# Issuing a differential-attention step's scores ahead of the value matmuls of the step two before it

## The reference, cut to what matters

```python
h = rms_norm(x, norm_w) * (1 + scale(c)) + shift(c)
u_a, v_a, z_a, q_b, k_b, v_b, z_b = split(h @ w_in)      # 2048 x 3584
a_out = gmlp_spatial_gating(u_a, v_a, ...) * silu(z_a)
# differential attention: 4 heads, each with two q/k parts of 64 and values of 128
q, k = rope(rms_norm(q_b)), rope(rms_norm(k_b))
s = q @ k.T * 64 ** -0.5 ; s = where(causal, s, -inf)     # for both parts
p = softmax(s)
a = p[part 0] - lam * p[part 1]
o = rms_norm(a @ v_b, subln_w) * (1 - lambda_init)
b_out = o * silu(z_b)
x = x + gate(c) * (concatenate([a_out, b_out]) @ w_out)
```

## Time and profile before

| | |
|---|---|
| time, median of 3 runs (lowest to highest) | 626.02 us (625.65 to 626.02) |
| the profiled execution's own time | 625.31 us |
| its span on the slowest core, core 1 | 624.3 us |
| spans of the other cores | 618.0 to 621.4 us |
| granted TensorE clock, core 1 / others, mean | 0.929 / 0.920 to 0.959 |
| TensorE busy with matmuls | 463.1 us (74%) |
| VectorE busy | 341.8 us (55%) |
| ScalarE busy | 319.5 us (51%) |
| exponentials (line 885) | 144, 155.9 us busy, 44.8 us idle before them |
| value matmuls (line 895) | 1088, 90.1 us busy, 33.7 us idle before them |
| score matmuls (line 848) | 576, 57.5 us busy, 21.7 us idle before them |

### The profile page before, as it was taken

One profiled execution on the slowest core, in us unless ns is written; L12 is line 12 of the kernel. 1 busy time (PEld: TensorE's weight loads), 2 busy tenths in 40 slices (PEclk: granted clock), 3 DMA queues, 4 the chain that ended last, 5 costly groups with the idle time before them and its releaser, 6 DMA issues.

```text
span 624.3 us, 9650 instructions; the slowest of 8 cores (618.0 to 624.3 us)
## 1 busy us (share of the span) xinstructions
PE 463.1 (74%) x3232; PEld 230.9 (37%) x3232; DVE 341.8 (55%) x755; ACT 319.5 (51%) x416; POOL 33.6 (5%) x38
## 2 busy tenths in 40 slices
PE   0022269999999999998986887587578768849990
PEld 0000024444444434344433454355355435424440
DVE  2153792156628878744687335633734644475555
ACT  1140557555336766762224888588679849600000
POOL 2010000000000000000453000000000000000000
PEclk9997569999999999999899999789989979979996
DMA  8999950312722040050002600000000000044777
GB/s 216 300 243 286 326 88 2 46 23 101 169 34 36 1 67 2 2 101 1 1 2 51 120 2 1 2 2 2 1 2 2 2 1 2 2 135 135 241 263 236
DMA packets 21696, 50.64 MB, mean 81 GB/s; under 512 B 1424, under 2 KB 8848, under 8 KB 21648
## 3 DMA queue, kind: packets, MB, share of 16 engines
q1 hardware_dynamic: 12656, 39.22, 19.3%
q0 software_dynamic: 8992, 10.81, 11.2%
HBM read 51.40 MB, written 8.39 MB: 96 GB/s over the span
## 4 chain that ended last, share of the span: by engine, by line
PE 47%; DMA 16%; DVE 14%; ACT 12%; issue 9%; SPq 1%; DVEq 1%; ACTq 0%
PE psum L666 17%; PE psum L613 9%; ACT sb_regA L885 8%; PE psum L895 7%; DVE sb_regD L559 4%; PE psum L848 4%; DMA sb_szb<-xT 3%; DMA out<-sb_regD 3%; DVE sb_regB L932 3%; DMA sb_regA<-xT 3%; DMA out<-sb_regA 3%; DMA sb_regD<-x 2%; PE psum L973 2%; PE psum L712 2%; DVE sb_regB L914 2%
## 5 line engine op out<-in xcount | busy, mean ns | idle before, releaser
L885 ACT ACTIVATE sb_regA<-psum,sb_small 128x1024 bf16<-128x1024 f32 x144 | 155.9, 1112 | 44.8 <-PE psum L848 26.1
L666 PE MATMUL psum<-sb_hT,sb_regC 128*128 128x512 bf16 x512 | 118.8, 385 | 5.2 <-ACT sb_hT L433 5.2
L895 PE MATMUL psum<-sb_vB,sb_regA 128*128 128x129 bf16 x1088 | 90.1, 226 | 33.7 <-ACT sb_regA L885 25.7
L895 PEld LDWEIGHTS psum<-sb_vB,sb_regA 128*128 128x128 bf16 x1088 | 67.7, 100 | 64.7 <-issue 64.5
L613 PE MATMUL psum<-sb_regC,sb_hT 128*128 128x512 bf16 x384 | 88.3, 383 | 0.0
L666 PEld LDWEIGHTS psum<-sb_hT,sb_regC 128*128 128x128 bf16 x512 | 50.5, 99 | 64.6 <-issue 9.8
L848 PE MATMUL psum<-sb_qT,sb_kT 64*128 64x256 bf16 (+1 forms) x576 | 57.5, 279 | 21.7 <-DVE sb_hT L870 16.0
L409 PE MATMUL psum<-sb_vB,sb_constb 128*128 128x512 bf16 x32 | 14.3, 626 | 67.0 <-ACT sb_vB L405 67.0
L613 PEld LDWEIGHTS psum<-sb_regC,sb_hT 128*128 128x128 bf16 x384 | 37.4, 99 | 45.2 <-issue 6.2
L906 DVE RECIPROCAL sb_fsm<-psum 128x4 f32<-128x4 f32 x32 | 5.8, 180 | 66.8 <-PE psum L895 66.8
L973 PE MATMUL psum<-sb_regC,sb_uz 128*128 128x512 bf16 x128 | 33.7, 387 | 0.0
(11 more groups left out here) (126 smaller groups left out, 518.8 us busy)
## 6 DMA issues: line engine op xcount, KB each, us to landing
sb_regD<-x SPq DMA_DIRECT2D x16, 512.0 KB, 5.7
sb_qT<-w_adaT SPq DMA_DIRECT2D x15, 512.0 KB, 10.4
sb_regC<-w_in POOLq DMA_DIRECT2D x7, 1024.0 KB, 11.5
sb_regD<-w_adaT SPq DMA_DIRECT2D x9, 512.0 KB, 12.7
out<-sb_regD SPq DMA_DIRECT2D x8, 512.0 KB, 4.1
out<-sb_regA SPq DMA_DIRECT2D x8, 512.0 KB, 3.9
sb_szb<-xT SPq DMA_DIRECT2D x1, 2048.0 KB, 21.4
sb_kT<-xT SPq DMA_DIRECT2D x1, 2048.0 KB, 21.9
```

Source lines behind the costliest of these rows:

```text
L666: P.op("pe", lambda E, kc=kc: E.matmul(PS(bank), lhsT=wslot[ws_][:, kc, 128 * c4:128 * (c4 + 1)], rhs=hT[:, kc, cols], start=(kc == 0), st ...
L885: P.op("act", lambda E: E.activation(out=et, in_=psum[:, X:X + 2, :], func=AF.Exp, bias=negM, scale=0.125), reads=[pb[X], pb[Y], b_small], ...
L895: P.op("pe", lambda E, u=u, j=j, c=c, i=i: E.matmul(psum[:, 2 * a + j, 256 * c:256 * c + 129], lhsT=et[:, c, QB * u + 128 * j:QB * u + 128 ...
```

## The change

The scores are issued two steps ahead. Before the loop both pairs of score banks are filled (`do_qk(0)`, `do_qk(1)`). Inside `do_exp_pv(gs)` the call `do_qk(gs + 2)` now stands after the exponential and after the transposes, if there are any, and before the value matmuls of `gs`. The loop's own `do_qk(gs + 1)` is gone. No instruction is added or taken away, and the queues of the other engines hold the same instructions in the same order.

```diff
@@ -886,6 +886,8 @@  (in do_exp_pv)
              reads=[pb[X], pb[Y], b_small], writes=[b_e[ei]])
         if tr_jq is not None:
             transposes(tr_jq, X)
+        if gs + 2 < NS:
+            do_qk(gs + 2)
         for u in range(2):
             i = 2 * kp + u
             for j in range(2):
@@ -938,10 +940,9 @@
     NS = len(gsteps)
     todo = []
     do_qk(0)
+    do_qk(1)
     for gs in range(NS):
         jq, h, kp, first, last = gsteps[gs]
-        if gs + 1 < NS:
-            do_qk(gs + 1)
         tr = None
         for item in list(todo):
             if item[0] == "r" and item[2] <= gs:
```

## The result

The changed kernel takes 611.46 us (median of 4 runs, 609.94 to 612.33), the kernel before 626.02 us beside it. The ratio is 0.9755, 95% interval 0.9721 to 0.979. The forecast was 611.6, in a range of 606.5 to 618.5. In a few executions of the experiments one die ran slower than the other at a lower granted clock (664 and 669 us in the two longest); the ratios leave them out.

A forecast was written before the change was run, and what follows sets the result against it. No engine was full: a chain through TensorE and ScalarE bound the even stretches, VectorE the block-pair changes. Savings of 5.1 - 1.4 + 3.6 + 3.6 + 3.5 = 14.4 us gave 611.6 us, range 606.5 to 618.5.

The forecast's parts named there:

- The chain and the new bound: Even stretches: two steps' chain falls from 2.33 to 1.78 us, below ScalarE's 2.02, so ScalarE sets 1.01 a step.
- The new wait in the first block pair: First block pair: values wait for their banks, with scores behind them; an exponential comes 0.4 to 0.7 us late, three times.
- Diagonal steps: Steps with a diagonal mask: second of two in a row about 0.2 us late, elsewhere 0.1 each, two per nine steps.
- The boundaries: Three block-pair changes: VectorE's 16.9 us stay and start later, 1.4 us lost in all; TensorE idles 6 to 8 us.
- Behind the first boundary: After the first block-pair change: low clock lasts until 409.89 and e-49 comes there both ways, TensorE's work being the same.
- The sum: Whole kernel: 14.4 us saved, span from 624.3 to 609.9 us, median time 611.6 us.
- the lowered clock under load: Rival: denser attention lowers TensorE's clock; at 0.81 a step takes 1.10 us, 9 us of gain gone, 620.5; chance 0.03.
- The longer low clock: Rival: after the boundaries the low clock lasts one stretch longer, costing 5 us, 616.5; chance 0.09.
- the steps stay short of ScalarE's rate: Rival: hand-overs between engines hold a step near 1.08 us, 7 us less gain, 618.5; chance 0.15.
- no effect: Rival: exponentials were held by something other than the order, time stays 626; chance 0.04.
- slower: Rival: clock stays at 1.2 GHz after the boundaries; 12 such steps a boundary lose 18.4 us, 630; chance 0.04.

The follow-up runs named there:

- the two runs with an extra operation: One more small ScalarE operation (128x8, result unused) behind each exponential: on the changed kernel 617.79 us (ratio 0.9871), on the kernel before 625.82 us (0.9993).
- The half order: Changed kernel with the scores of s+2 between two halves of the value matmuls of s (four values, scores, four values): 622.79 us, ratio 0.9937.
- The spread kernels: VectorE's sixteen multiplications per block pair spread over the next three rounds, transposes in the fourth: on the kernel before 612.39 us, on the changed kernel 590.52 us.

## Why the prediction was right, point by point

**The chain and the new bound: right.** The 0.20 us waits are gone, a step takes 1.008 us on average against 1.01, and the two runs with an extra operation show ScalarE as the bound after and not before. The half order shows the rest of the chain: plain steps of 1.037 with 0.28 us ahead. The idle before the exponentials came at 34.0 us, not about 30; on the slowest core 0.1 of it is in the even stretches and 29.7 at and behind the boundaries.

**The new wait in the first block pair: right in place and size.** The first values of a group wait for VectorE's last read of the bank (0.62 + 0.19 us at 373.11 and 373.57), and one exponential is late after it, by 0.56 to 0.58 us three times; I took 0.6.

```profile
373.11 0.27 PE L897 MATMUL psum<-sb_vB,sb_regA 128*128 128x129 bf16 x2 [0.62 <-DVE sb_regB L916]
373.54 0.29 DVE L921 SCALAR_TENSOR_TENSOR sb_regB<-sb_regB 128x128 f32<-128x128 f32 x1
...
373.57 0.50 PE L897 MATMUL psum<-sb_vB,sb_regA 128*128 128x129 bf16 x6 [0.19 <-DVE sb_regB L916]
```

**Diagonal steps: too dear.** I took 0.2 for two in a row and 0.1 for each other one. In ScalarE's timeline most steps take 0.996 us and those around a mask 1.02 to 1.06, so a diagonal costs some 0.06 over a plain step. The 1.01 that I read from pairs is that of the first step after a wait, a little slower than the rest; the two errors meet, and nine steps with two diagonals take 9.08 us (e-54 to e-63 on core 2), just 9 x 1.01. My extra 0.1 to 0.2 is 0.6 us too much in each of the two long stretches (25.8 forecast, 25.2 measured) and about as much in the first block pair.

**The boundaries: right in time.** Nothing was won there. They grew by 0.4, 0.5 and 0.4 us (20.0, 20.8, 16.9), for 0.5, 0.3 and 0.5 taken, as VectorE's 16.90 us start that much later. The spread kernels show that this chain was the bound. TensorE's wait for the copy did not come as written, 6 to 8 us at each: it is 6.4 at the second and third (5.8 and 6.0 before), but 4.02 at the first, against 4.27. There TensorE idles 2.14 us for ScalarE before it and does most of the groups between the two idles at 1.2 GHz. The end does not move by that, since VectorE sets it.

**Behind the first boundary: wrong.** I wrote that e-49 comes at the same time both ways, as TensorE's work until then is the same. The work is, but its idle is not. The value matmuls that used to run in the wait for the second copy now run before the transposes, and that wait grows from 0.72 to 1.36 us. At a low clock TensorE is the bound, so it is not made up: 8.2 for 7.5. Where the clock came back before e-49, on three cores, it is 7.6 to 7.7. The other two boundaries, where I did count this, came at 4.7 and 6.2 for 4.6 and 6.2.

**The sum was right partly by cancelling.** The forecast is core 1's path with the start and the output stage as they were; the slowest core after is core 2. Its attention takes 183.8 us for 184.9 forecast, 1.1 us less, but its e-1 starts at 342.71 and not at 341.25, 1.5 us later; from e-143 to the end the two cores take the same (83.7). That gives a span of 610.2 for 609.9 forecast. Which core enters the attention last and how late is not a thing that I forecast, so that the two nearly cancel is luck, about 1 us of it.

**The rivals.** In the profiled executions the lowered clock under load did not come: TensorE busy 23.68 of 25 us at a clock of 1.00, against 19.93. The 13/16 limit that the Trainium skill ("TensorE: Matmul & The Clock Gate", section "Seeing it yourself") describes shows neither here nor in the output stage of the kernel before, where all eight cores had TensorE busy 29.8 to 30.0 of 30 us (570 to 600 us) at a clock of 1.00. The longer low clock came on some cores, for 2.1 us. That the steps stay short of ScalarE's rate is refuted by the 27 exponentials in a row, no effect and slower by the time.

## What to carry to other kernels

When two buffers alternate between a producer and a consumer, the in-order queue of the producer should hold first what refills the buffer just freed, and then what merely uses the consumer's result: both wait for the same event, and only one of them is on the loop. Compute the loop for two steps with and without the instructions in between, and compare it with the busiest engine's two steps; half a move may leave most of the loss, since masks, a group's first step and waits for a third engine eat the margin.

Where another engine's chain sets the pace, such a reorder gains nothing, and it can lose: there the old order filled a stall. Look for those places first, keep the old order in them, and then shorten that chain, as spreading the multiplications and placing the transposes did for 22 us more.

## What the runs showed of the hardware

- An exponential over 128x1024 is recorded with 1.11 us, but in plain steps the next one starts 0.996 us after it (1.008 on average over 27 in a row, masks included); with the 128x8 operation between them it is 1.09 to 1.10, so that costs 0.10 us, though its own record says 0.20.
- After an idle of 4 to 6.4 us TensorE works at 1.2 GHz for a while, and how long differs from core to core in one execution: in the ten microseconds from 1 us before e-80 on, the eight cores of the changed kernel's profiled execution had a mean clock between 0.50 and 0.85, with the same instructions. The one at 0.50 took 2.1 us more for e-82 to e-107 than the others (27.3 for 25.2).
- ScalarE's queue brought a wait that I had not foreseen: the small activation of line 928 (926 before) waits 1.50 us for VectorE at the first boundary, where it waited 0.31 before, and the exponential behind it keeps TensorE idle 2.14 us. Soon after that, still before the long stall, eight value matmuls take 0.98 us, which is the low clock. It cost nothing here, since VectorE bound that stretch: its 16.90 us are unchanged.
